# A sixteen-expert layer's last pair reaches its tokens by TensorE in two rounded parts, and the row fetches are spread over the layer's end

## The reference, cut to what matters

```
pg = softmax(t @ w_rg + b_rg)                # top 1 of 4 groups
pe = softmax(le_sel);  top 2 of 4 experts    # two experts a token
w  = p_top * pe_top / sum(pe_top)
act = silu(t @ w_gate[e]) * (t @ w_up[e]) * gates[t, e]
y   = sum over e of act @ w_down[e]          # e: 16 experts of width 256
x   = x + m[5] * y                           # m[5]: a gate row, one for prompt, one for latent tokens
```

## Time and profile before

| | |
|---|---|
| three runs | 1564.82, 1563.63, 1559.85 us; median 1563.63 |
| the profiled execution | 1559.05 us, its span 1557.2 us |
| busy share of the span | PE 92%, weight loads 47%, DVE 49%, ACT 21%, POOL 6% |
| granted clock of PE, mean | 0.959 of full speed |
| moved by DMA | 436.84 MB, mean 281 GB/s |

### The profile page before, as it was taken

The page is one execution under the profiler, slowest core; times in us unless marked ns, Lnnn a source line. Parts: engine busy times, 40 slices in busy tenths (PEclk is TensorE's granted clock), DMA queues, the critical chain, the costliest instruction groups (busy, mean ns, idle before and its releaser), DMA issues. The chain is left out here.

```text
span 1557.2 us, 17818 instructions
## 1 busy us (share of the span) xinstructions
PE 1428.9 (92%) x6473; PEld 738.9 (47%) x6473; DVE 765.3 (49%) x1849; ACT 323.5 (21%) x705; POOL 86.1 (6%) x97
## 2 busy tenths in 40 slices
PE   5998998999678999799999999999998998989985
PEld 3334535444245444456666666454443446454432
DVE  1334205553566544566666666036445455156434
ACT  1104304111223111511111111032112125131101
POOL 0000010000220001000000000010001010100001
PEclk9999999999889999999999999989999999979998
DMA  9989968899895998745555554646998730049995
GB/s 358 386 313 370 387 235 324 344 423 422 328 354 226 417 422 346 271 135 178 177 179 176 180 177 140 230 181 263 420 423 339 292 115 1 27 187 401 424 422 227
DMA packets 152277, 436.84 MB, mean 281 GB/s; under 512 B 6945, under 2 KB 63105, under 8 KB 123137
## 3 DMA queue, kind: packets, MB, share of 16 engines
q1 hardware_dynamic: 136816, 396.93, 66.8%
q10 hardware_dynamic: 11920, 26.24, 4.4%
q0 software_dynamic: 3456, 12.58, 2.3%
HBM read 414.20 MB, written 21.53 MB: 280 GB/s over the span
## 5 line engine op out<-in xcount | busy, mean ns | idle before, releaser
L1002 PE MATMUL bank<-gate_up_weights,hT_gathered 128*64 128x512 f32 (+1 forms) x1280 | 255.1, 598 | 15.4 <-SPq L542 14.3
L840 PE MATMUL bank<-panel,hT 128*128 128x512 f32 x384 | 168.2, 597 | 5.1 <-DVE hT L1241 4.2
L1002 PEld LDWEIGHTS bank<-gate_up_weights,hT_gathered 128*64 128x64 f32 (+1 forms) x1280 | 82.8, 132 | 180.1 <-issue 179.6
L1016 PE MATMUL bank<-down_weights,actT 128*64 128x512 f32 (+1 forms) x640 | 138.5, 603 | 2.5 <-ACT actT L2145 2.5
L1426 DVE SCALAR_TENSOR_TENSOR ada_sums<-panel,cond_columns,ada_sums 128x384 f32<-128x384 f32 x224 | 121.1, 609 | 0.0
L840 PEld LDWEIGHTS bank<-panel,hT 128*128 128x128 f32 x384 | 73.4, 192 | 94.5 <-issue 88.6
L651 PE MATMUL bank<-panel,hT 128*128 128x512 f32 x240 | 107.0, 604 | 3.4 <-DVE hT L1241 2.5
L987 PE MATMUL bank<-h_hi,P 128*128 128x512 f32 x216 | 95.2, 441 | 3.5 <-DVE h_lo L1615 3.5
L987 PE MATMUL bank<-h_lo,P 128*128 128x512 f32 x216 | 88.2, 408 | 0.0
L651 PE MATMUL bank<-panel,oT 128*128 128x512 f32 x192 | 84.3, 595 | 1.3 <-ACT oT L2054 1.3
L2132 ACT ACTIVATE silu<-bank 128x256 f32<-128x256 f32 x36 | 13.9, 385 | 320.0 <-PE bank L1002 320.0
(11 more groups left out here) (330 smaller groups left out, 1923.8 us busy)
## 6 DMA issues: line engine op xcount, KB each, us to landing
gate_up_weights<-in_gate_up_halves SPq DMA_DIRECT2D x148, 1024.0 KB, 13.3
down_weights<-in_down_rows SPq DMA_DIRECT2D x74, 1024.0 KB, 13.5
panel<-in_w_ada SPq DMA_DIRECT2D x27, 2048.0 KB
panel<-in_w_ada SPq DMA_DIRECT2D x16, 1536.0 KB
ada_panel_third<-in_w_ada SPq DMA_DIRECT2D x9, 2048.0 KB
y_by_slot<-y_rows ACTq DMA_DIRECT2D x32, 512.0 KB, 8.1
panel<-in_ret_w_in SPq DMA_DIRECT2D x16, 1024.0 KB
panel<-in_attn_w_qkv SPq DMA_DIRECT2D x5, 2048.0 KB
```

The costliest lines, as they stand in the source:

```text
L840: last = PE.matmul(ps[t][:], hT[:, k, t * 128:(t + 1) * 128], panel[f % 2][:, k, :], start=k == 0, stop=k == KD - 1)
L1002: last = PE.matmul(ps[2][width * s:width * s + width, :], hg[:, j, k, width * s:width * s + width], gu_ring[w][:, 2 * k // KD, :, k % (KD ...
L1016: last = PE.matmul(ps[6 + half][width * s:width * s + width, :], actT[:, c, width * s:width * s + width], dn_ring[w][:, c, half * 512:half ...
```

## The change

1. Row 7 is not stored any more. `fetched` is 896 slots, so tokens of experts 14 and 15 that sit in slots read the row of zeros. Row 7 goes by PE as row 8 does.
2. Both rows' results are multiplied with the slot's weight in the same DVE instruction as with the gate row (`weighted_row`), and are split in two parts in the format of the gather matmuls (float32r): the high part is an ACT copy (`y_hi`), the low part a DVE subtraction (`y_lo`). PE multiplies both with a table of ones (`hots`), made by DVE from the transposed table: 24 float32r matmuls (`pe_last_rows`) instead of six in float32, which the trace records as twelve.
3. The six fetches go into four places, each fetch behind a gate of its own: 0 when rows 0 to 6 are stored, 1 after row 7's gate-up, 2 after row 8's transposes, 3 after take 1, 4 after row 8's gate-up, 5 after take 2. Takes 0 and 1 stand ahead of row 8's activation, takes 2 to 4 behind it and ahead of row 8's results, take 5 behind these. None is left in `tail`.
4. ACT waits at the start of each layer but the first until all six sums of the layer before are done. Buffers have moved to make room.

```diff
-    ytok = [tmp_row, ybuf[:, 1, :], hgt[:], hg_rows[:, 1, :], tmp_row, hg_rows[:, 0, :]]
+    ytok = [tmp_row, hg_rows[:, 1, :], hgt[:], hg_rows[:, 1, :], hg_rows[:, 0, :], hgt[:]]
+    Y_BUFFER = (0, 1, 2, 1, 0, 2)
...
+    def pe_last_rows(pe, l):
+        pe.wait_ge(sem("row_y_lo"), 3 * l + 1)
+        for pair, t in ((1, 0), (1, 1), (0, 0), (1, 2), (0, 1), (0, 2)):
+            hot, parts = ((hot8, (y_hi8, y_lo8)), (hot7, (y_hi7, y_lo7)))[pair]
+            for half in range(2):
+                if not pair and t == 0:
+                    pe.wait_ge(sem("row_y_lo"), 3 * l + 2 + half)
+                for i, part in enumerate(parts):
+                    last = PE.matmul(ps[2 * t + half][:], hot[:, t * 128:(t + 1) * 128], part[:, half * 512:half * 512 + 512],
+                                     start=bool(pair) and i == 0, stop=not pair and i == 1)
+                if not pair:
+                    last.then_inc(sem("unit_sum"), 1)
...
+        if q == PAIRS - 1:
+            pe.wait_ge(sem("row_weights"), 2 * l + 1)
+            pe_table_T().then_inc(sem("row_PT"), 1)
...
+        def hot_table(l, q):
+            n = 2 * l + q - (PAIRS - 1) + 1
+            dve.wait_ge(sem("row_PT"), n)
+            step(V.tensor_reduce(slot_weight(q), ps[4][:, 0:T], AX.X, ALU.add))
+            V.tensor_scalar(hots[q - (PAIRS - 1)][:], ps[4][:, 0:T], 0.0, None, ALU.is_gt).then_inc(sem("row_hot"), 1)
+
+        def weighted_row(n, q, half, into):
+            o = slice(half * 512, half * 512 + 512)
+            dve.wait_ge(sem("row_down"), 2 * n + half + 1)
+            V.scalar_tensor_tensor(into[:, o], ps[6 + half][:], slot_weight(q), grow[:, o], ALU.mult, ALU.mult)\
+                .then_inc(sem("row_y"), 1)
...
             if q < PAIRS:
                 row_gathered(l, q + 1)
+            if q == PAIRS - 1:
+                hot_table(l, q)
...
         def last_row(l):
             n = ROWS * l + PAIRS
-            weigh(0, slice(0, 4), "unit_weights")
+            weigh(0, slice(0, 4), "row_weights")
             dve.wait_ge(sem("row_y"), 2 * n)
             step(V.scalar_tensor_tensor(grow[:], gdiff[:], latent[:, PAIRS:ROWS], moe_gate[:, 0, :], ALU.mult, ALU.add))
+            take(l, 0)
+            take(l, 1)
             dve.wait_ge(sem("row_silu"), n + 1)
             dve.wait_ge(sem("row_actT"), n)
             V.tensor_tensor(act[:], ps[2][:, FE:2 * FE], silu[:], ALU.mult).then_inc(sem("row_act"), 1)
+            take(l, 2)
+            hot_table(l, PAIRS)
+            dve.wait_ge(sem("row_y_hi"), 3 * l + 1)
+            V.tensor_tensor(y_lo7[:], ybuf[:, 1, :], y_hi7[:].bitcast(F), ALU.subtract).then_inc(sem("row_y_lo"), 1)
+            take(l, 3)
+            take(l, 4)
             dve.wait_ge(sem("y_stored0"), 16 * 4 * (l + 1))
             for half in range(2):
-                take(l, half)
+                weighted_row(n, PAIRS, half, ybuf[:, 0, :])
                 o = slice(half * 512, half * 512 + 512)
-                dve.wait_ge(sem("row_down"), 2 * n + half + 1)
-                V.tensor_tensor(ybuf[:, 0, o], ps[6 + half][:], grow[:, o], ALU.mult).then_inc(sem("row_y"), 1)
-            take(l, 2)
-            take(l, 3)
+                dve.wait_ge(sem("row_y_hi"), 3 * l + 2 + half)
+                V.tensor_tensor(y_lo8[:, o], ybuf[:, 0, o], y_hi8[:, o].bitcast(F), ALU.subtract).then_inc(sem("row_y_lo"), 1)
+            take(l, 5)
...
         for l in range(depth):
+            if l:
+                e.wait_ge(sem("unit_sum"), 2 * TILES * l)
...
                 if i == 1:
+                    pool.wait_ge(sem("row_gateup"), ROWS * l + PAIRS)
+                elif i == 2:
+                    pool.wait_ge(sem("row_hT"), 2 * (ROWS * l + PAIRS) + 2)
+                elif i == 3:
+                    pool.wait_ge(sem("y_used"), 2 * TILES * l + 2)
+                elif i == 4:
+                    pool.wait_ge(sem("row_gateup"), ROWS * (l + 1))
                 elif i == 5:
-                    pool.wait_ge(sem("row_gateup"), ROWS * (l + 1))
+                    pool.wait_ge(sem("y_used"), 2 * TILES * l + 3)
```

More of the change, by code:

```diff
@@ L1077, in pe_row @@
                     last = PE.transpose(ps[5][0:KD, i * 128:(i + 1) * 128], mods[:, v * KD:(v + 1) * KD, i % 2], ident)
-            last.then_inc(sem("unit_PT"), 1)
+            last.then_inc(sem("row_PT"), 1)
             pe.wait_ge(sem("units_known"), l + 1)
@@ L1108, in pe_more @@
         for k in range(KD):
-            last = pe_gateup(pe, 1, k, (2, 3, 0, 1))
+            last = pe_gateup(pe, 0, k, (2, 3, 0, 1))
         last.then_inc(sem("o_gateup"), 1)
@@ L1119, in pe_more @@
         atleast(pe, "o_copied", 5 * n + 5)
-        pe_scatter(pe, hgt, ybuf[:, 1, :], lambda half: atleast(pe, "o_y", n + 1), "o_sum")
+        pe_scatter(pe, hgt, hg_rows[:, 0, :], lambda half: atleast(pe, "o_y", n + 1), "o_sum")
         atleast(pe, "o_step", 6 * n + 6)
@@ L1158, in _ @@
             pe.sem_inc(sem("quads_done"), 1)
-            pe.wait_ge(sem("unit_PT_sb"), l + 1)
-            pe_scatter(pe, lpart, ybuf[:, 0, :], lambda half: pe.wait_ge(sem("row_y"), 2 * ROWS * (l + 1) - 1 + half), "unit_sum")
+            pe.wait_ge(sem("row_hot"), 2 * l + 2)
+            pe_last_rows(pe, l)
         for half in range(2):
@@ L1733, in row @@
                 o = slice(half * 512, half * 512 + 512)
-                dve.wait_ge(sem("row_down"), 2 * n + half + 1)
-                V.tensor_tensor(ybuf[:, q % 2, o], ps[6 + half][:], grow[:, o], ALU.mult).then_inc(sem("row_y"), 1)
+                if q == PAIRS - 1:
+                    weighted_row(n, q, half, ybuf[:, 1, :])
+                else:
+                    dve.wait_ge(sem("row_down"), 2 * n + half + 1)
+                    V.tensor_tensor(ybuf[:, q % 2, o], ps[6 + half][:], grow[:, o], ALU.mult).then_inc(sem("row_y"), 1)
                 if half == 0 and q < PAIRS:
@@ L1815, in tail @@
             units_in(l, 0, 1)
-            take(l, 4)
+            units_in(l, 1, 0)
             mean_square(n, 0)
-            units_in(l, 1, 0)
-            if l + 1 < depth:
-                scale_low(n, 0)
             units_in(l, 1, 1)
@@ L1823, in tail @@
                 final(0)
-            take(l, 5)
-            mean_square(n, 1)
-            if l + 1 == depth:
                 units_in(l, 2, 0)
+                mean_square(n, 1)
                 units_in(l, 2, 1)
@@ L1832, in tail @@
                 return
+            scale_low(n, 0)
+            units_in(l, 2, 0)
+            mean_square(n, 1)
+            units_in(l, 2, 1)
             scale_low(n, 1)
             evacuate(l + 1, 0, 0)
-            units_in(l, 2, 0)
-            units_in(l, 2, 1)
             mean_square(n, 2)
@@ L2128, in row @@
             n, par = ROWS * l + q, q % 2
+            if q == PAIRS:
+                e.wait_ge(sem("y_used"), 2 * TILES * l + 1)
+                e.wait_ge(sem("row_y"), 2 * n)
+                S.activation(y_hi7[:], ybuf[:, 1, :], ACT.Copy).then_inc(sem("row_y_hi"), 1)
             e.wait_ge(sem("row_gateup"), n + 1)
@@ L2135, in row @@
             else:
[L2136 removed]
                 if 1 <= l < depth - 1:
[L2138 to L2139 removed]
+                    e.wait_ge(sem("row_PT"), 2 * l + 2)
+                    S.activation(mpan[0:KD, :], ps[5][0:KD, :], ACT.Copy).then_inc(sem("gate_rows"), 1)
                 e.wait_ge(sem("units_known"), l + 1)
@@ L2147, in row @@
                 if 1 <= l < depth - 1:
-                    e.wait_ge(sem("unit_PT_sb"), l + 1)
+                    e.wait_ge(sem("gate_rows"), l)
                     e.dma_start(gate_rows.rearrange("v c (k f) -> k (v c) f", f=128), mpan[0:KD, :].rearrange("p (g f) -> p g f", f=128))\
                         .then_inc(sem("gate_rows_stored"), 16)
+                e.wait_ge(sem("y_used"), 2 * TILES * l + 4)
+                for half in range(2):
+                    o = slice(half * 512, half * 512 + 512)
+                    e.wait_ge(sem("row_y"), 2 * n + half + 1)
+                    S.activation(y_hi8[:, o], ybuf[:, 0, o], ACT.Copy).then_inc(sem("row_y_hi"), 1)
                 return
             row_turned(l, q + 1)
+            if q == PAIRS - 1:
+                return
             e.wait_ge(sem("row_y"), 2 * n + 2)
```

57 lines of the change are left out of this document (37 added, 20 removed).

## The result

The changed kernel takes 1587.67 us, median of four runs (1583.39 to 1588.72), beside 1562.0 us for the kernel before, median of four (1559.85 to 1564.82). The ratio is 1.0158, 95% interval 1.0131 to 1.0185: 25.7 us slower. The forecast was 1575 with a range of 1564 to 1585, so the direction was right, the median lies 2.7 us above the range, and the loss is twice the 12.9 us of the sum. The profiled execution has a span of 1586.9 us and a mean granted clock of 0.95.

A forecast was written before the change was run, and what follows sets the result against it. Each layer's end was taken as a chain on VectorE, then ScalarE, only then PE. Layer terms -1.6 + 5.7 + 3.9 + 4.9 gave +12.9 us: 1572 on the profiled execution, 1576.5 on the median; predicted 1575, range 1564 to 1585.

The forecast's parts named there:

- Takes 0 and 1 fit ahead of the activation: During row 8's gate-up (starting at E): takes run from about E+4.6 to E+7.5, just ahead of the activation at E+7.94.
- Three transposes shift E by 0.33: On PE in row 7: three table transposes delay E, the start of row 8's gate-up, by 0.33 us in layers 0 to 2.
- U at E+21.1, 22.1, 22.1 and 21.8: Layer ends 0 to 3: VectorE's first add of PE's sums (U), timed from row 8's gate-up start (E); before, 16.78 to 21.86.
- After the last low part PE has fourteen float32r matmuls left, 14 x 0.23 = 3.2 us at the pitch of the earlier trace: PE's sums at a layer's end: the last fourteen matmuls take 3.2 us, and ScalarE's first square waits for them.
- rival 2: PE's clock falls: fourteen matmuls at half clock in layers 0 to 2, each end 3.2 us later, 1584; chance 0.14.
- From the square to the mixer 6.9 us, to the third tile's scaling 8.4: Layer ends: after the first square starts, tile 0's hT is ready 6.9 us later, the third tile's scaling starts near 8.4.
- with nothing to spare: Layer 0's end: the pooling table's transfer, issued 13 us later, lands some 10 to 12 us after issue, just before wanted.
- What follows is dense and passes on whole: PE after the layer ends: shifts of -1.6, +5.7 and +3.9 us in layers 0, 1 and 2 pass on whole.
- Layer 3's weights 2.4 us later: Layer 3 before row 8's gate-up: fetches move 1.0 MB more while PE waits for weights, delaying it 2.4 us.
- Layer 3's own chain: Layer 3's end: VectorE's first add 21.8 us after row 8's gate-up start, against 17.88 (+3.9); the tail loses 1.4 of 9.97.
- Rival 3: In layers 1 and 2 panel landings, not VectorE, end the stage: -3.5 us, 1559.5; chance 0.07.

The follow-up runs named there:

- e2: The changed kernel with 21 unread matmuls added in TensorE's two pauses before row 8's sums: 1584.55 us, ratio 1.0124.
- e3: The changed kernel with the first table in its own place and ScalarE waiting for the sums only before tile 2's square: 1572.37 us, ratio 1.0065.
- e4: The changed kernel with layer 3's fetches held until row 8's second gate-up weights have landed: 1586.49 us, ratio 1.0141.
- e9: The changed kernel with unread matmuls in layers 0 to 2's pauses and around tile 0's turns in layers 1 to 3: 1572.28 us, ratio 1.0062.
- e5: The changed kernel with row 8's result ahead of takes 3 and 4, plus the edits of e3 and e4: 1563.15 us, ratio 1.0013.

## Why the prediction was right or wrong

1. *Takes 0 and 1 fit ahead of the activation*: right. In layers 0 to 2 they ran from E+3.8 or 4.2 to E+7.5 at the latest, and the activation stood at E+7.6.
2. *Three transposes shift E by 0.33*: they can't be told apart. E of layer 0 was 391.47 to 395.47 us in e2, e3 and e4, whose instructions up to there are those of the changed kernel, so the 2.1 us of the first piece lies within this spread.
3. *U at E+21.1, 22.1, 22.1 and 21.8*: right, it was 21.57, 22.42, 22.55 and 22.40. Take 4 started at E+14.5 in layer 0 and E+15.4 and 15.5 in layers 1 and 2, for 14 and 15.
4. *"After the last low part PE has fourteen float32r matmuls left, 14 x 0.23 = 3.2 us at the pitch of the earlier trace rows"*: this is the step that failed. They took 6.1 to 6.4 us in layers 0 to 2, at 0.43 us each and a granted clock of 0.51, so the first square stood at E+27.0, 28.2 and 27.5 instead of E+23.5, 25.8 and 24.1. In layer 3, where the pauses were 1.66 and 1.32 us, they took the 3.2. The rows to see it were shown: the earlier trace rows has a clock of 0.50 behind such a pause. And the argument against rival 2 compared the wrong thing: the 4.47 us of the earlier trace rows are VectorE's wait for a fetch. TensorE's own pauses in layer 0 before were 2.07 and 3.32 us, no longer than those to come, and the clock fell behind them:

```profile
406.11 1.10 PE L1048 MATMUL bank<-y_rows,logit_parts 128*128 128x512 f32 x2 [2.07 <-issue]
410.53 6.85 PE L1048 MATMUL bank<-y_rows,logit_parts 128*128 128x512 f32 x10 [3.32 <-DVE y_rows L1753]
```

   I took the new pauses to be "about 2 us", but the times gave a longer one: row 8's down matmuls ended at E+12.6 in the trace before, so row 7's eight matmuls end near E+14.7 with the shift of E+0.33, and the first low part, by the two round trips of 4.4 us ending at E+19.7 or 20.7, comes near E+17.5 or 18.5. That is 3 to 4 us; 3.42, 4.18 and 4.11 were measured.
5. *From the square to the mixer 6.9 us, to the third tile's scaling 8.4*: right, 6.65 and 6.50, and 8.48. So steps 3 and 5 with the clock of e9 give nearly the forecast: there s is at E+25.1, 26.4 and 25.4, and the mixer at E+33.1 and 31.9 for 32.7 and 31.0. e9's time, 1572.3, is near the forecast too, but also holds what it saved on the panels. In layer 0 the third tile was scaled at E+35.5 for a forecast of E+31.9, 3.6 of the 4.5 us by which its piece was missed. The pooling table didn't come "with nothing to spare": issued at 420.03, it landed 7.2 us later, and VectorE first read it at 434.43.
6. *What follows is dense and passes on whole*: wrong by 1.0 us in layer 1, where tile 0's sixteen panel matmuls took 9.87 us instead of 8.86, more of them at half clock. A further 1.4 us between there and layer 2's E has no cause that I can show; the other kernels differ there by -2.3 to +1.5 us from before, e3 by the most.
7. *Layer 3's weights 2.4 us later*: the mechanism was right, the size was off. The wait was 18.13 instead of 14.30 us, 3.8 more; e4 shows that all four fetches of 2.1 MB count, 5.1 us. I had counted 1.9 MB now against 0.9 before, 2.4 us between them; the 12.99 of e4, where no fetch and no store of row 7 moves, lies only 1.3 below the 14.30 of before. By the Trainium skill ("DMA: Bandwidth & Descriptors", Queues, rings and completion order) each DMA engine takes turns between its queues; the trace agrees, since the weights lost what the fetches moved.
8. *Layer 3's own chain*: U 0.6 us later than forecast, since the gate-up took 9.68 us, more of it at half clock than before (8.52; granted clock 0.73 over it, 0.83 before); the end stood 8.8 us behind U with its last output instruction, as forecast (8.6).
9. *Rival 3's time*: its own terms give -3.5 us, which by the way of the other rivals' times is 1558 and not 1559.5. Nothing hangs on it.

What each cause is worth depends on what else is in place: the order 19.4 us, the clock 15.4, ScalarE's wait 15.3, each taken away alone. They shorten the same chain and must not be added; e5 shows it for the first and the third.
